# Expert layer of a two-block transformer on one core: weight columns read in steps of four in the up products, and the hidden rows turned by two full transpositions

## The reference

```python
w1: (32, 1024, 512)   w3: (32, 1024, 512)   w2: (32, 512, 1024)
def expert_block(args):
    xblk, e = args
    return (jax.nn.silu(xblk @ w1[e]) * (xblk @ w3[e])) @ w2[e]
```

## Time and profile before

| | us |
|---|---|
| median of 3 runs | 1862.56 |
| the profiled execution's own time | 1863.68 |
| its span | 1861.9 |
| PE busy in the span | 1722.3 (93%) |
| DVE busy / ACT busy | 711.2 / 596.3 |
| the 32 experts' stage on PE | about 467 to 957 |

### The profile page before, as it was taken

One profiled execution on the slowest core, in us unless ns is written; L12 is line 12 of the kernel. 1 busy time (PEld: TensorE's weight loads), 2 busy tenths in 40 slices (PEclk: granted clock), 3 DMA queues, 4 the chain that ended last, 5 costly groups with the idle time before them and its releaser, 6 DMA issues.

```text
span 1861.9 us, 24887 instructions
## 1 busy us (share of the span) xinstructions
PE 1722.3 (93%) x10485; PEld 1315.9 (71%) x10485; DVE 711.2 (38%) x1523; ACT 596.3 (32%) x1052; POOL 169.0 (9%) x128
## 2 busy tenths in 40 slices
PE   7999999996999888878889999998999899999998
PEld 5878766885655554545558967766787798888886
DVE  4355444453111111211136467665734542322223
ACT  3434354423010000000125456554624432222222
POOL 1000110220111111101101000011001000000221
PEclk9999999998999999999999999998999999999999
DMA  7512100348899999999995331012520222223201
GB/s 260 179 46 91 46 23 23 123 193 325 329 400 409 412 417 400 404 409 408 415 354 188 119 111 66 1 46 101 182 91 12 91 102 91 90 84 138 96 23 45
DMA packets 79005, 341.91 MB, mean 184 GB/s; under 512 B 7943, under 2 KB 15751, under 8 KB 65448
## 3 DMA queue, kind: packets, MB, share of 16 engines
q1 hardware_dynamic: 73192, 329.76, 45.9%
q0 software_dynamic: 5120, 8.40, 1.3%
q10 hardware_dynamic: 576, 2.10, 0.3%
HBM read 329.75 MB, written 18.87 MB: 187 GB/s over the span
## 4 chain that ended last, share of the span: by engine, by line
PE 70%; DMA 18%; DVE 5%; ACT 4%; issue 2%; POOL 0%; SPq 0%; ACTq 0%; DVEq 0%; POOLq 0%
PE ps L552 66%; DMA arenaf<-in_w 14%; DMA arenaf<-in_mem 2%; PE ps L971 1%; PE ps L2848 1%; PE ps L2039 1%; DMA hd<-junk 1%; ACT splitr L628 1%; DVE arenaf L2930 1%; DVE splitr L617 0%; PE ps L806 0%; ACT arenaf L867 0%; DVE arenaf L2948 0%; DMA arenaf<-yd 0%; ACT arenaf L960 0%
## 5 line engine op out<-in xcount | busy, mean ns | idle before, releaser
L552 PE MATMUL ps<-hr,splitr 128*128 128x512 f32 (+1 forms) x2784 | 580.7, 368 | 6.7 <-POOL hr L903 4.3
L552 PEld LDWEIGHTS ps<-hr,splitr 128*128 128x128 f32 x2784 | 477.9, 193 | 89.4 <-issue 4.9
L552 PE MATMUL ps<-splitr,hr 128*128 128x512 f32 (+1 forms) x1488 | 273.7, 343 | 2.3 <-DVE hr L1068 1.4
L552 PEld LDWEIGHTS ps<-splitr,hr 128*128 128x128 f32 x1488 | 234.2, 190 | 35.9 <-issue 2.5
L617 DVE TENSOR_TENSOR splitr<-ring,splitr 128x2048 fp32r<-128x2048 f32 x61 | 142.8, 2343 | 231.4 <-ACT splitr L628 231.3
L628 ACT CAST splitr<-ring 128x2048 fp32r<-128x2048 f32 x61 | 116.1, 1904 | 152.0 <-PE ps L552 142.8
L2071 DVE TENSOR_TENSOR arenaf<-arenaf,ps 128x256 f32<-128x256 f32 x32 | 13.5, 421 | 267.3 <-PE ps L552 240.7
L2106 ACT COPY junk<-ps 64x512 f32<-64x512 f32 x32 | 18.5, 579 | 293.6 <-PE ps L552 293.6
L552 PE MATMUL ps<-arenaf 128*64 128x128 f32 (+7 forms) x784 | 103.0, 342 | 5.5 <-ACT arenaf L978 3.6
L552 PE MATMUL ps<-arenaf,tq 128*64 128x512 f32 x336 | 84.8, 650 | 22.0 <-DMA arenaf<-in_w 22.0
L617 DVE TENSOR_TENSOR splitr<-arenaf,splitr 128x2048 fp32r<-128x2048 f32 x27 | 62.2, 2303 | 106.0 <-ACT splitr L628 106.0
(11 more groups left out here) (391 smaller groups left out, 1967.7 us busy)
## 6 DMA issues: line engine op xcount, KB each, us to landing
ring<-in_w SPq DMA_DIRECT2D x22, 2048.0 KB, 44.2
arenaf<-in_w SPq DMA_DIRECT2D x22, 2048.0 KB, 43.9
splitf<-in_w SPq DMA_DIRECT2D x21, 2048.0 KB, 44.0
hf<-in_w SPq DMA_DIRECT2D x20, 2048.0 KB, 44.2
ring<-in_w_in SPq DMA_DIRECT2D x11, 2048.0 KB, 10.9
otf<-in_w SPq DMA_DIRECT2D x11, 2048.0 KB, 45.0
ring<-in_w_gate_up SPq DMA_DIRECT2D x7, 2048.0 KB, 8.0
arenaf<-in_w_in SPq DMA_DIRECT2D x4, 2048.0 KB, 9.1
```

The lines of the kernel that those rows point to most:

```text
L552: return te.matmul(out, lhsT, rhs, start=start, stop=stop)
```

## The change

The halves of the up products no longer take neighbouring columns. Half h reads the weight columns 4c + 2h and 4c + 2h + 1, for c = 0 to 127: two runs of 128 columns, each in steps of four elements (16 bytes). The result has the same size and stands in PSUM without gaps. So `HROW` holds in its first 128 columns the hidden columns 4c (upper half: 4c + 2), and in the next 128 the columns 4c + 1 (4c + 3). Turning one block of 128 columns over all 128 partitions gives two of the four blocks of `HCOL` at once. `pe_down` picks them in the order 0, 2, 1, 3.

```diff
@@ pe_up
-                            it = mm(ps[CAP * half:CAP * half + CAP, 0:256], XTF[:, k, :],
-                                    W[:, k, 256 * half:256 * half + 256], k == 0, k == 7)
+                            it = mm(thirds(ps[CAP * half:CAP * half + CAP, 0:256], 2), XTF[:, k, :],
+                                    W[:, k, :].rearrange("p (c q) -> p q c", q=4)[:, 2 * half:2 * half + 2, :],
+                                    k == 0, k == 7)
@@ pe_turn_hidden
-                for k in range(4):
-                    for half in range(2):
-                        a = CAP * half
-                        it = mm(ps[a:a + CAP, CAP * k:CAP * k + CAP], HROW[a:a + CAP, k:256:4],
-                                ident[a:a + CAP, a:a + CAP], True, True)
+                for j in range(2):
+                    it = te.transpose(ps[:, 128 * j:128 * j + 128], HROW[:, 128 * j:128 * j + 128], ident)
@@ pe_down
-                        it = mm(ps[CAP * half:CAP * half + CAP, :], HCOL[:, k, :],
+                        it = mm(ps[CAP * half:CAP * half + CAP, :], HCOL[:, k % 2 * 2 + k // 2, :],
```

## The result

| | median us | runs | lowest to highest |
|---|---|---|---|
| before | 1863.14 | 4 | 1860.45 to 1868.63 |
| after | 2002.16 | 4 | 2001.19 to 2005.51 |

The ratio is 1.075 (95% interval 1.073 to 1.077): the change makes the kernel 139 us slower. The profiled execution has a span of 1999.5 us against 1861.9, 137.6 more.

The account below looks back on a forecast made before the run. The expert stage was taken to be bound by weight transfers, 6 MB per expert, not by PE. 1863.68 - 0.5 + 0.4 = 1863.6, less 1.1 to the median, gave 1862.5 us; range 1856 to 1885.

Parts of the forecast that it names:

- rival A: Up products: moving reads go at half speed, 7.0 us per product, PE becomes the bound; +122 us, 1985 us; chance 0.16.
- the up products with steps of four: Term for the stepped weight reads: 0 to +3.5 us per product, taken as +0.4, hidden except at the first product.
- the near row: Estimate from stationary loads with a step, 0.94 against 0.84 ns per column (12%): +0.4 us per up product.
- the far end: Upper estimate for up products: two halves share a port that gives stepped reads at half rate, +3.5 us per product.
- rival B: Expert stage: PE's saving counts where it has no waits, or throughout; up to 24 us saved, 1839 us; chance 0.04.
- The 0.5 us that I granted the end: Stage's end: of the last turn's 0.75 us saving, only the last down product's lag behind its landing is usable, -0.5 us.
- The turning itself: Hidden rows: two 128x128 transpositions replace eight products, saving 0.75 us of PE per expert, 24 us over 32 experts.
- The cover: Middle of the expert stage: PE's wait for weights hides extra PE work, 12.8 us of PE against 15.43 of transfers.
- Break-even: Up products: the cover ends at 1.7 us extra per product, when one takes 1.49 times as long.
- The first product: Stage's start: the first load waits for the first up product with the queue empty, so its loss delays all landings, +0.4 us.
- Rival C: Expert stage: stepped PE reads touch more memory lines and slow the transfers; 2% is 9.6 us, 1872 us; chance 0.04.

Follow-up runs that it names:

- e5: Kernel before with the up products' two loops exchanged, so one column half runs after the other, without a step: 1923.8 us (one run).
- e6: Changed kernel with the up products' two loops exchanged, so one half runs after the other, in steps of four: 2288.15 us (one run).
- e2: Changed kernel with up products reading columns in steps of two and the hidden rows turned by reads in steps of two: 1866.26 us, ratio 1.0010.
- e3: Changed kernel with each half reading pairs of neighbouring columns out of every four, hidden rows turned in steps of two: 1868.24 us, ratio 1.0022.
- e8: Changed kernel with steps of three in both up products, over 384 of the 512 columns: 1889.06 us (one run), 5.46 us per product.
- e9: Changed kernel with steps of eight in both up products, over pairs of weight rows: 2008.03 us (one run), 7.37 us per product.
- e10: Kernel before with token rows turned from 128 neighbouring columns instead of every eighth: 1859.43 us (one run), eight loads in 0.58 us instead of 0.96.
- e4: Changed kernel with the up products' former reads of 256 neighbouring columns, so only the turning is new: 1865.59 us, ratio 1.0009.
- e7: Changed kernel with steps of four in the w1 product alone, w3 reading neighbouring columns: 1884.84 us against 1866.67, ratio 1.0095.

## Why the prediction was wrong

The forecast was 1862.5 us and "no change"; the result is 2002 us, slower by 7.5%. It was rival A that came true, at a chance of 0.16, and the range, 1856 to 1885, did not hold it.

**The step that failed** is "the up products with steps of four", where I bounded a moving read by stationary reads the earlier trace rows, took the near row, +0.4 us per product, and kept +3.5 as the far end. It measured +3.75 us. The far end came close by luck, since its mechanism was wrong: no port is shared (e5, e6), each stream pays for its own lines (e2, e3, e8, e9). (Its 2.4 columns per ns are 512 / 219 = 2.3; nothing else hangs on them.)

**Why the near row misled.** I compared loads of 128 columns with a step (0.96 us for eight) to those of L2149 without one (1.73 us for sixteen, 0.84 ns per column) and read 12%. e10 gives the right partner, the same eight loads without a step: 0.58 us. The step makes them 1.7 times as long. The L2149 loads were no measure of a load: each stands beside a moving operand of 128 columns, the token rows beside one of 64. In the trace the first two L2149 loads start 57 ns apart and all later ones 109 to 111, which is 0.85 ns per moving column, the pace of the up products. That the loads there were paced by this moving side is my reading of these rows, no run took it apart. What e10 shows is that the trace of before held a slowed load where I saw an unslowed one.

**The Trainium skill's rule.** The Trainium skill, Advanced Engine Details and Errata, section "Memory Cachelines", asks for at least two hits on each line of 16 bytes. The runs agree with that: two hits cost 5% (e2, e3), one hit 107%. The Trainium skill, SBUF — State Buffer, in its section on the DMA port swizzle, has a stride of up to 4 fp32 free. The measurement decides against that (2.07 times). I weighed the rule against rows that did not test it, and gave it too little.

**The bound.** The reading held that the stage hangs on the transfers and not on PE. e4 takes 0.74 us per expert off PE and gains nothing (1.0009), and rival B falls. The 0.5 us that I granted the end is below what the runs can tell. The turning itself, 0.75 us saved, measured 0.74.

**The cover.** Break-even was put at 1.49 times an up product's duration. e8 at 1.56 costs 1889.06 against 1866.67, 22 us. e7, 15.8 us of PE against 15.43 of transfers, costs 18. Both lie above the threshold (e7's two products together take 1.54 times as long), and at 1.05 (e2, e3) nothing is lost. No run lies between, so the place of 1.49 is borne out by e7's sum and not measured. The cost just above it is larger than 29 x the excess: once the cover is gone, the turn of the tokens of `mem` and the waits behind it count too (e7), which the prediction had not looked at.

**Rival A's price** was 122 us and 1985. The product takes 7.25 us and not 7.0, which makes an expert 19.55 us and not 19.0: 0.55 x 29 = 16 us more.

**The first product** cost 1.7 us at the issue of the first load and not what a stepped product costs elsewhere (3.75), since PE's clock stood at its lower level there and the product without a step was slow too (5.73).

**Rival C**, slower transfers, did not come to bear. In e7, with half of the reads in steps, PE is busy all the time and the queue still moves 405 GB/s:

```profile
700.00:800.00 100.00, 100.00 (x566) 43.24 (x566) 16.08 (x46) 8.11 (x20) 12.99 (x14) 1.00 1.01 405
```

In the changed kernel the matrices land ahead of PE, so that slower ones could not cost anything there. Whether its transfers are slowed a little stays open: a share of 0.92 for 338 GB/s is 9% more busy time per byte than the 1.01 for 406 of before, and e5, which has no steps and in which PE is the bound too, shows 4% (0.99 for 382, from 500 to 600 us).

## What to carry to other kernels

A pattern that saves instructions on one operand can cost on another: before a float32 matmul's moving operand is given a step, count how many elements it takes out of each 16 bytes. For float32, steps of two or pairs of four did the same reordering here for 5% (the turning's stationary read, in steps of two, took over the rest), and steps of four doubled the product. If only a bound from another kind of read is at hand, check that the row for the plain case is limited by the read itself, and let the range follow the far end while the near one is unproven. And where the transfers bound a stage, work taken off PE buys nothing, while work put on it costs as soon as the cover ends. Here 139 us lost stood against a possible gain, by my own sum, of 0.5.

## What the runs showed of the hardware that I had not expected

- At the lower clock a stepped product is hardly slower than at full clock: 7.49 us for the stage's first one against 7.42 later. The clock was granted at 0.50 and 0.64 of full speed in these windows of the changed kernel. The product without a step went from 5.73 to 3.6. In the trace its pairs of records start 0.427 us apart at the lower clock and 0.216 at the full one. Those of the stepped product start 0.45 us apart at either. I read this as a pace set by the reads and not by the array's clock.

```profile
462.00:464.00 2.00, 1.41 (x6) 0.72 (x8) 0.54 (x1) 0.00 (x0) 0.94 (x1) 0.50 0.00 0
464.00:468.00 4.00, 4.00 (x20) 1.77 (x18) 0.00 (x0) 0.00 (x0) 0.00 (x0) 0.64 0.22 59
```

- The two column halves of the array gain a full factor of 2 where they run side by side: a stream's records start 0.216 us apart alone (e5) and 0.219 beside the other, with steps of four 0.451 (e6) and 0.453. Exchanging the loops costs only a factor of 1.65 (5.8 against 3.5 us) and 1.63 (11.8 against 7.25), since successive halves still overlap by about four records at each joint.
- The first up product starts at 462.5 to 464.1 us in some of these programs and at 466.2 to 469.3 in others, though they do not differ ahead of it. The means of the two groups are 4.4 us apart. That is part of why single runs of kernels with no effect stand at 1858 and at 1866.
